# Two expert stages on one core: the extra blocks split around the first block's gate and up products

## The reference, cut to what matters

```python
# first block: top 2 experts of 32, hidden width 256
(jax.nn.silu(xb @ w_gate[e]) * (xb @ w_up[e])) @ w_down[e]
...
# second block: top 4 experts of 32, hidden width 1024, with biases and clamps
gu = xe @ w_gu[e] + b_gu[e]
x_glu = jnp.minimum(gu[:, :D_FF], SWIGLU_LIMIT)
x_lin = jnp.clip(gu[:, D_FF:], -SWIGLU_LIMIT, SWIGLU_LIMIT)
act = (x_lin + 1) * (x_glu * jax.nn.sigmoid(SWIGLU_ALPHA * x_glu))
return act @ w_dn[e] + b_dn[e]
```

## Time and profile before

| what | value |
|---|---|
| median of 3 runs | 1977.44 us (1976.01 to 1978.85) |
| the profiled execution | 1975.73 us, span 1973.9 us, mean granted TensorE clock 0.978 |
| PE busy | 1793.9 us, 91% of the span |
| DVE, ACT busy | 522.7 us, 394.9 us |
| data moved | 626.81 MB, mean 318 GB/s |
| chain that ended last | PE 59%, DMA 32% |
| stage 1 (8 groups) | about 404 to 687 us |
| stage 2 (32 experts) | about 995 to 1963 us |
| further blocks that ran | 2 in stage 1, 2 in stage 2 |

### The profile page before, as it was taken

How to read it: one execution, slowest core, us unless ns; L and a number is a source line. 1 busy time by engine, 2 the same in 40 slices (tenths; PEclk the granted TensorE clock), 3 DMA queues, 4 the chain that set the end, 5 groups by cost and what they waited for, 6 DMA issues and landing times.

```text
span 1973.9 us, 27226 instructions
## 1 busy us (share of the span) xinstructions
PE 1793.9 (91%) x10815; PEld 988.7 (50%) x10816; DVE 522.7 (26%) x1208; ACT 394.9 (20%) x912; POOL 51.0 (3%) x109
## 2 busy tenths in 40 slices
PE   7999999986867999899999999998897999989987
PEld 4766777754544667678743333333333333333332
DVE  4685331132212240342541111111111111111112
ACT  3343552021101220433111110011110111101111
POOL 0040000000000010100010000000000000000000
PEclk9999999998978999999999999999999999999999
DMA  9979315439999752423466999999999799999996
GB/s 398 409 268 394 138 65 216 168 150 394 422 411 413 303 109 93 84 59 102 167 261 257 428 427 428 427 429 427 429 427 428 292 427 428 428 428 428 427 428 284
DMA packets 57691, 626.81 MB, mean 318 GB/s; under 512 B 7360, under 2 KB 11456, under 8 KB 13472
## 3 DMA queue, kind: packets, MB, share of 16 engines
q1 hardware_dynamic: 55744, 620.09, 76.2%
q0 software_dynamic: 1584, 4.33, 2.1%
q10 hardware_dynamic: 272, 1.05, 0.1%
HBM read 624.39 MB, written 1.05 MB: 317 GB/s over the span
## 4 chain that ended last, share of the span: by engine, by line
PE 59%; DMA 32%; DVE 3%; issue 3%; ACT 2%; DVEq 0%; SPq 0%; ACTq 0%
PE ps L500 57%; DMA ring<-in_w_gu_dram 27%; DMA ring<-in_moe_w_gate_dram 4%; PE ps L667 2%; DMA ring<-in_w_dn_dram 1%; ACT arena L1549 1%; ACT arena L1720 1%; DMA hN<-in_x_dram 1%; DVE stat L2114 0%; DVE arena L2131 0%; SPq L525 0%; PE ps L663 0%; DVEq L1992 0%; DVE hN L2007 0%; DVE rstd L1963 0%
## 5 line engine op out<-in xcount | busy, mean ns | idle before, releaser
L500 PE MATMUL ps<-ring,arena 128*64 128x512 f32 (+2 forms) x4416 | 734.9, 553 | 97.7 <-DMA ring<-in_w_gu_dram 48.5
L500 PEld LDWEIGHTS ps<-ring,arena 128*64 128x64 f32 (+1 forms) x4416 | 242.6, 128 | 534.6 <-issue 418.0
L500 PE MATMUL ps<-arena 128*32 128x256 f32 (+13 forms) x2434 | 382.6, 452 | 38.3 <-ACT arena L1549 15.5
L500 PEld LDWEIGHTS ps<-arena 128*64 128x64 f32 (+8 forms) x2434 | 171.2, 146 | 225.3 <-issue 157.7
L500 PE MATMUL ps<-hT,ring 128*128 128x256 f32 (+1 forms) x960 | 236.1, 401 | 5.0 <-DVE hT L2040 2.0
L500 PEld LDWEIGHTS ps<-hT,ring 128*128 128x128 f32 x960 | 179.4, 191 | 60.5 <-issue 35.6
L1549 ACT ACTIVATE arena<-ps 128x512 f32<-128x512 f32 (+4 forms) x191 | 104.7, 571 | 312.2 <-PE ps L500 178.2
L2385 DVE TENSOR_SCALAR arena<-ps 128x512 f32<-128x512 f32 (+1 forms) x34 | 23.0, 676 | 509.5 <-PE ps L500 509.5
L1815 ACT ACTIVATE arena<-ps,mod,gain 128x128 f32<-128x128 f32 x176 | 66.1, 458 | 422.4 <-PE ps L500 422.4
L1827 ACT ACTIVATE arena<-arena 128x512 f32<-128x512 f32 (+1 forms) x44 | 25.3, 575 | 567.4 <-DVE arena L2385 375.9
L500 PEld LDWEIGHTS ps<-arena,hN 128*128 128x128 f32 x896 | 104.6, 193 | 32.4 <-issue 18.0
(11 more groups left out here) (306 smaller groups left out, 908.3 us busy)
## 6 DMA issues: line engine op xcount, KB each, us to landing
ring<-in_w_gu_dram SPq DMA_DIRECT2D x96, 2048.0 KB, 25.5
ring<-in_w_dn_dram SPq DMA_DIRECT2D x64, 2048.0 KB, 21.4
arena<-in_w_gu_dram SPq DMA_DIRECT2D x32, 2048.0 KB, 27.3
ring<-dense_dram SPq DMA_DIRECT2D x56, 1024.0 KB, 8.9
ring<-in_moe_w_up_dram SPq DMA_DIRECT2D x16, 2048.0 KB, 15.7
ring<-in_moe_w_down_dram SPq DMA_DIRECT2D x16, 2048.0 KB, 15.0
ring<-in_ada_w_dram SPq DMA_DIRECT2D x24, 1024.0 KB, 18.0
ring<-in_w_mod_dram SPq DMA_DIRECT2D x24, 1024.0 KB, 7.8
```

Of the source, the lines that this page charges most:

```text
L500: ins = nc.tensor.matmul(*a, start=start, stop=stop, **k)
```

## The change

The further blocks of both stages are cut in two. `run_experts` now takes four parts and runs them in this order: gate and up of the further blocks, gate and up of the first block, down and scatter of the further blocks, down of the first block. The turned activation of a further block can't stay in `actT`, so ACT copies it to a place of its own for each block (`kept`), and later copies it back into a new buffer `actM`, from which PE reads. The making, turning and copying of the further block's second one-hot matrix move into its second part. In stage 2 PE also waits there for the first block's activation, because the turn goes into bank 1. SP's order and its waits are unchanged.

```diff
+        actM = M(256)
+        kept = {1: hflat[:, 2048:2048 + 256 * (MAXB[1] - 1)], 2: biasB[:, 1536:1536 + 256 * (MAXB[2] - 1)]}
...
                     with eng.If(more > 0):
                         with eng.Fori(0, more) as b:
-                            further(it, u, g, before + b, b + 1)
-                    first(it, u, g)
+                            further_hidden(it, u, g, before + b, b)
+                    first_hidden(it, u, g)
+                    with eng.If(more > 0):
+                        with eng.Fori(0, more) as b:
+                            further_down(it, u, g, before + b, b)
+                    first_down(it, u, g)
...
# PE, stage 1
                     hidden_group(it, u, x, xsM1, False)
-                    pe.wait_ge(x["spread_onehot"], q + 1)
-                    spread_turn(x, ohsM, 3, T)
                     occupy(7, 4, True)
                     pe.wait_ge(x["act"], q + 1)
                     act_turn(2, x)
                     pe.wait_ge(x["actT"], q + 1)
+
+                def further_down(it, u, p, q, b):
+
+                    pe.wait_ge(x["spread_onehot"], q + 1)
+                    spread_turn(x, ohsM, 3, T)
                     pe.wait_ge(x["spread"], q + 1)
-                    down_group(it, u, x)
+                    pe.wait_ge(x["actT_back"], q + 1)
+                    down_group(it, u, x, actM)
                     pe.wait_ge(x["ys"], q + 1)
                     scatter_group(x, ysM1, ohtM)
...
# PE, stage 2
                     act_turn(2, x)
+                    pe.wait_ge(x["actT"], q + 1)
+
+                def further_down(it, u, e, q, b):
+
+                    pe.wait_ge(s["act"], e + 1)
                     pe.wait_ge(x["spread_onehot"], q + 1)
                     spread_turn(x, ohsM, 1, 0)
-                    pe.wait_ge(x["actT"], q + 1)
+                    pe.wait_ge(x["actT_back"], q + 1)
                     down_strips(it, u, x)
...
# ACT: block_of(...) becomes four parts; of the further block's two:
+                def further_hidden(it, u, e, q, b):
+                    if n == 1:
+                        act_.wait_ge(x["gathered"], q + 1)
+                        half_out(x, 1, xsM1, 2)
+                    act_.wait_ge(x["glu"], q + 1)
+                    a(sg[:, 0:256], glu[:, 0:256], ACT.Sigmoid, scale=1.702 if n == 2 else 1.0).then_inc(x["sig"], 1)
+                    act_.wait_ge(x["turned"], q + 1)
+                    copy(kept[n][:, bass.ds(b * 256, 256)], ps[:, 3, 0:256]).then_inc(x["actT"], 1)
+
+                def further_down(it, u, e, q, b):
+                    act_.wait_ge(x["spreadT"], q + 1)
+                    copy(ohtM, ps[:, 3, T:2 * T] if n == 1 else ps[:, 1, 0:T]).then_inc(x["spread"], 1)
+                    act_.drain()
+                    copy(actM, kept[n][:, bass.ds(b * 256, 256)]).then_inc(x["actT_back"], 1)
...
# DVE
+                def further_hidden(it, u, e, q, b):
+                    gather_onehot(x, ohgM, e, more_slots(b))
                     v.wait_ge(x["gathered"], q + 1)
                     pair_out(x, xsM1) if n == 1 else xs_out(x, xsM, q + 1)
                     units(x, q + 1)
+
+                def first_hidden(it, u, e):
+                    units(s, e + 1)
+
+                def further_down(it, u, e, q, b):
+                    spread_onehot(x, ohsM, e, more_slots(b))
                     v.wait_ge(x["down"], q + 1)
                     ys_out(x, ysM, ysM1)
```

More of the change, by code:

```diff
@@ L471, in program, with run_experts @@
         gates_used = sem("moe1_gate_weights_used")
-        def run_experts(eng, n, further, first, begin=lambda *_: None):
+        def run_experts(eng, n, further_hidden, first_hidden, further_down, first_down, begin=lambda *_: None):
             with eng.Fori(0, E // GROUP[n] // 2) as it:
@@ L1211, in down_group @@
                         for x in range(4):
-                            last = mm(ps[32 * x:32 * x + 32, 3 * half, :], actT[:, f, x * 32:(x + 1) * 32],
+                            last = mm(ps[32 * x:32 * x + 32, 3 * half, :], turned[:, f, x * 32:(x + 1) * 32],
                                       w[x][:, f, half * 512:(half + 1) * 512], start=f == 0, stop=f == 1)
@@ L1331, in moe1 @@
                 pe.wait_ge(madeV, nth(madeV, ("tables", 1)))
-                run_experts(pe, 1, further, first, begin)
+                run_experts(pe, 1, further_hidden, first_hidden, further_down, first_down, begin)
                 pe.wait_ge(s["ys"], E // GROUP[1] + 1)
@@ L1394, in moe2 @@
                 pe.wait_ge(madeV, nth(madeV, ("tables", 2)))
-                run_experts(pe, 2, further, first, begin)
+                run_experts(pe, 2, further_hidden, first_hidden, further_down, first_down, begin)
                 pe.wait_ge(s["ys"], E + 1)
@@ L1827, in block_of, with first_down @@
                     a(sg[:, 0:w], glu[:, 0:w], ACT.Sigmoid, scale=1.702 if n == 2 else 1.0).then_inc(s["sig"], 1)
-                    if n == 1 and s is not x:
-                        act_.wait_ge(s["gathered"], q + 1)
+                def first_down(it, u, e):
+                    w = 512 if n == 2 else 256
+                    if n == 1:
+                        act_.wait_ge(s["gathered"], e + 2)
                         half_out(s, 1, xsP, 2)
-                    act_.wait_ge(s["turned"], q)
+                    act_.wait_ge(s["turned"], e + 1)
@@ L1832, in block_of @@
                     copy(actT.rearrange("p a b -> p (a b)")[:, 0:w], ps[:, 3, 0:w]).then_inc(s["actT"], 1)
-                    if second is not None:
-                        act_.wait_ge(s["gathered"], second * 2 + 4)
+                    if n == 2 and u == 1:
+                        act_.wait_ge(s["gathered"], it * 2 + 4)
                         half_out(s, 1, xsP, 0)
-                    act_.wait_ge(s["spreadT"], q)
-                    copy(onehotT, ps[:, 3, T:2 * T] if n == 1 else ps[:, 1, 0:T]).then_inc(s["spread"], 1)
+                    act_.wait_ge(s["spreadT"], e + 1)
@@ L1839, in moe @@
+                    copy(ohtF[u % 2], ps[:, 3, T:2 * T] if n == 1 else ps[:, 1, 0:T]).then_inc(s["spread"], 1)
                 if n == 2:
@@ L2393, in moe, with more_slots, further_hidden @@
                 slots0 = cst("time", 1, SLOTS[n] + 1)
-                def further(it, u, e, q, b):
-                    slots = cst("time", 1)[:, bass.ds(b * MORE + (SLOTS[n] - MORE), MORE)]
-                    gather_onehot(x, ohgM, e, slots)
-                    spread_onehot(x, ohsM, e, slots)
+                def more_slots(b):
+                    return cst("time", 1)[:, bass.ds(b * MORE + SLOTS[n], MORE)]
+                def further_hidden(it, u, e, q, b):
+                    gather_onehot(x, ohgM, e, more_slots(b))
                     v.wait_ge(x["gathered"], q + 1)
@@ L2435, in moe @@
                 gather_onehot(s, ohgF, n, slots0, n)
-                run_experts(v, n, further, first)
+                run_experts(v, n, further_hidden, first_hidden, further_down, first_down)
             moe_front(1)
```

37 lines of the change are left out of this document (17 added, 20 removed).

## The result

| | median of runs | lowest to highest | profiled execution | its span |
|---|---|---|---|---|
| before | 1976.76 us (4 runs) | 1976.01 to 1978.85 | 1975.73 | 1973.9 |
| changed | 1996.53 us (4 runs) | 1995.41 to 1999.56 | 1997.11 | 1994.9 |

The ratio is 1.0097, 95% interval 1.0082 to 1.0111: the changed kernel is 1.0% slower, some 20 us. The forecast was 1998.0. The total is where it was put; the shares that make it are not all, and that is what most of the following is about.

A forecast was written before the change was run, and what follows sets the result against it. Weight transfers set stage 2's time, with the end fixed by chunk 4's issue. Terms 5.5 + 5.5 + 8.5 + 1.3 = 20.8 us on 1975.73 gave 1996.5, put at 1998 us against the median; range 1983 to 2010.

The forecast's parts named there:

- Chunk 4 decides: Stage 2: transfers restart for good when the further block's down chunk 4 is freed; earlier gate and up release gains 0.
- The stall in stage 2: Before the further block's turn PE idles 5.0 us for DVE, then 0.95 for two copies; stalls some 6.0 us.
- Block one: Stage 2's first further block: stalls 6.0 plus slow clock 2.5, so chunk 4 comes 8.5 us later.
- Block two: Stage 2's second further block: 8.5 us less 7.2 for the old stall and slow clock, 1.3 us later.
- The clock: Down products behind new idle time run at half clock: plus 2.5 us in stage 2, 1.8 in stage 1.
- 2.9 + 1.1 − 0.3: Stage 1 further blocks: idle 2.9 us, turn and copies 1.1, one copy saved 0.3; with the clock 5.5, twice.
- Plain groups: Stage 1 groups without further blocks: one more compare and branch per engine, counted as 0.
- rival 3: Stage 1: one more 3.45 us instruction stall in each of six plain groups, plus 21, 2019 us; 6%.
- its mirror: Stage 1: shorter jumps and a group's instruction stall gone, some 4 us at most, 1994 us; 7%.
- The front: Unchanged code up to stage 1's first gate and up products: forecast 0.

The follow-up runs named there:

- the filler kernel: Changed kernel plus products with zeros in PE's new stalls (18 and 3 in stage 2, 10 and 3 in stage 1): 1987.52 us, ratio 1.0048.
- the runs with either stage alone: Changed order in one stage only, the other whole as in the kernel before: stage 1 alone 1984.86 us, ratio 1.0027; stage 2 alone 1988.24 us, ratio 1.0049.
- the padded ones: Changed kernel plus never-run products in the part of stage 1 that plain groups jump over: 128 products 2018.73 us, ratio 1.0193; 64 products 2019.02 us, ratio 1.0212.

## Why the prediction was right, and where it was not

**Chunk 4 decides: right.** Both blocks end with empty transfers, chunk 4 to the end is constant to 0.5 us, and delaying gate and up left chunk 4 where it was. I had not seen that a still later release costs 3 us behind each block.

**The stall in stage 2: right.** Idle 5.0 forecast, 4.57 found; copies 0.95 and 1.06; down products 2.5 over, 2.4 found. Block one 8.5 and 8.5. Block two 1.3 and 2.4: idle time and slow clock of the new stall came out 1.3 us smaller there (4.58 and 1.63 us), but a term of 2.1 us was missing. PE came 2.34 us early for a gate and up chunk, where it waits 1.95 us in the kernel before, and the clock fell behind it, `1537.10 3.61 PE` for 32 products that took 1.93 us in the filler kernel after a wait of 2.33 us. This is mostly the change and not chance: all eleven executions with stage 2 split have that wait at 2.31 to 2.34 us, and nine of them ran the products behind it in 2.72 to 3.61 us; the two with stage 2 whole have 1.95 and 1.96 us and ran them in 1.93. Why the wait is longer with the split stays open.

**The clock: right in stage 2, a matter of the execution in stage 1.** I took 1.8 us for each of its two blocks, between 0 and 3.7. In group 0 of the profiled execution the clock did not fall at all after 2.58 us of idle time (3.64 us for the down products): 4.3 us instead of 5.5. In four other executions with the same idle time it fell, and these products took 5.34 to 5.91 us, near the 1.8 over. In the last group it fell twice, behind a wait of 2.02 us for the up chunk and again behind 2.39 us at the turn: 10.7 instead of 5.5, of which 2.0 is that wait, 1.7 and 2.7 the slow clock, and 3.5 the two idle times. In the same four other executions it held at the turn, or nearly: behind 2.37 to 2.39 us of idle time the products took 3.64 to 3.81 us. (A slip in the sum: 2.9 + 1.1 − 0.3 is 3.7 and not 3.8, and with the clock's 1.8 that gives the 5.5.)

**Plain groups: this is the step that failed.** The prediction gave groups without a further block 0, had rival 3 for one stall more, and allowed its mirror "some 4 us at most, since the transfers bind soon after". By the marks of the table they gave 9.8. Stalls for instructions fell by 11.6 us and waits for weights rose by 7.2; the other 5 to 6 us are PE's busy time, 125.7 and 119.8 us for the same products, at mean granted clocks of 0.82 and 0.86. That the transfers bind was right, and more strictly than the bound had it: it counted a pass at 58.8 us, the rate of stage 2, but here they moved 416 to 421 GB/s, and 181 us for three passes is what they took before and after. What the prediction left out is PE's lag behind them. The kernel before came to the up weights of the last group 6.8 us after they had landed. With fewer stalls PE had caught up, and since only PE's work is left in the last group, these some 6 us count in full, though no transfer got faster. The other 3.7 of the 9.8 us came straight back in the last group, as its wait of 2.02 us for the up chunk and 1.7 us of slow clock behind that. The split of the 9.8 is worked out from rows; that the shorter stretch comes with the split of stage 1 is shown by the runs with either stage alone, and that code which is only jumped over moves the stalls by the padded ones. The Trainium skill, "Runtime: NRT & Kernel Launch", section "Instruction fetch mechanics", says that a taken branch out of what is loaded stalls. The traces agree so far as every stall of the table lies right behind a jump or within 33 products of one; that the branch itself causes it no run here isolates. The same section's store of 2048 instructions does not by itself explain why a loop of some 1850, counted from the code, is fetched anew in each pass while one of 1460 stays.

**The front: not in the sum.** 3.4 us in code that both kernels share. At 162 us, the kernel before and then the changed one:

```profile
162.00:164.00 2.00, 2.00 (x22) 0.72 (x16) 1.83 (x5) 0.48 (x1) 0.00 (x0) 1.00 1.13 418
```

```profile
162.00:164.00 2.00, 2.00 (x12) 0.42 (x8) 1.84 (x5) 0.00 (x0) 0.00 (x0) 0.50 1.04 434
```

The clock fell in one and not in the other, 1.7 us, and once more near 199 us. In the experiments the first gate and up products begin between 415.1 and 422.2 us, so one profiled pair can't tell 3 us there from nothing.

So the total of 1996.5 came out because −9.8 in the plain groups was made up by +5.2 too much in the last group and +3.4 in the front. The part that was understood, stage 2, is 9.8 us forecast and 9.7 measured alone, though block two reached its 2.4 us by a term that was not in the sum. The part that was lucky is stage 1, 11.0 forecast, 5.4 measured alone. The two runs add to 15.1 us and the whole change is 1.0% or 19 us by its ratio; with intervals of 3 to 4 us on each that is no contradiction, and no proof that they add.

## What to carry to other kernels

Splitting a block to free its first weights early helps only if those weights are the ones that the next transfers wait for: look which chunk's release ends the empty time in the transfers, and count everything up to that. When a part is moved behind another, list what each engine has between the two; here DVE's activation and one-hot lay bare, and moving the put-off scatter and gather into that place turned a loss of 20 us, together with the earlier one-hot, into a gain of 5. In a loop that is fetched anew in each pass, an edit can change the time of passes that don't run it: compare the stretches that the edit doesn't touch before you ascribe the total to the edit. And where transfers set the pace, cut a stretch at landings as well as at issues: an issue says how far the engine is, a landing how far the weights are.

## What the hardware showed that I had not expected

64 products behind a condition that is never true made the kernel 1.1% slower than the changed kernel (ratios 1.0212 and 1.0097), and 128 did no more than that. The same idle time was followed by either level of the granted clock: behind 2.58 us in group 0 it fell in four of five executions (32 products in 5.34 to 5.91 us instead of 3.64), behind 2.37 to 2.39 us in the last group in one of five, and behind 2.31 to 2.34 us in block two in nine of eleven (32 products in 2.72 to 3.61 us instead of 1.93). Behind 3.01 us and behind 4.57 it fell each time. So for idle times like these one execution does not tell what the clock costs, and a sum should carry it as a range.
